# Recurrence output stored once in float32 and split where it is loaded, and a gates' slab loaded ahead of the block's moves

## What is computed

```
u_lru, g_lru, q, k, v, gate_lru, gate_attn = split(x @ w_in + b_in)
u     = depthwise_conv(u_lru)
h     = scan of h[t] = a[t] * h[t-1] + bt[t], forward and backward; a and bt from gates(u)
y_lru = ((h_fwd + h_bwd) * gelu(g_lru)) @ w_lru_out          # D_RNN = 1280
y_att = windowed_gqa(q, k, v) @ w_attn_out
mix   = (sigmoid(gate_lru) * y_lru + sigmoid(gate_attn) * y_att) @ w_o
x     = layer_norm(ALPHA * x + mix)
out   = layer_norm(ALPHA * x + gated MLP(x))                 # D_FF = 3072
```

## Time and profile before

| | us |
|---|---|
| median of 3 runs | 2767.41 (2765.99 to 2768.99) |
| the profiled execution | 2770.9 |
| its span (first to last instruction) | 2769.1 |
| PE busy in the span | 2671.8 |
| phase lru of q = 0 | about 0 to 376 |
| phase lru of q = 1 | about 1845 to 2024 |

### The profile page before, as it was taken

One profiled execution on the slowest core, in us unless ns is written; L12 is line 12 of the kernel. 1 busy time (PEld: TensorE's weight loads), 2 busy tenths in 40 slices (PEclk: granted clock), 3 DMA queues, 4 the chain that ended last, 5 costly groups with the idle time before them and its releaser, 6 DMA issues.

```text
span 2769.1 us, 32046 instructions
## 1 busy us (share of the span) xinstructions
PE 2671.8 (96%) x11898; PEld 2202.5 (80%) x11898; DVE 1506.4 (54%) x1800; ACT 753.4 (27%) x1033; POOL 654.1 (24%) x332
## 2 busy tenths in 40 slices
PE   8997999999899999999999999989999999999998
PEld 6886788888678877888888888878788778888886
DVE  7899864334313657745445464667742314644445
ACT  4565713313210022010101011148831211211112
POOL 3554531231133612334343433310000000000000
PEclk9998999999899999999999999999999999999999
DMA  6565654444686833434343534357756794544554
GB/s 232 183 204 185 213 193 160 172 157 159 262 353 231 301 125 137 137 137 153 136 179 128 188 124 161 132 215 235 244 186 228 256 343 159 205 183 182 192 201 168
DMA packets 174272, 535.67 MB, mean 193 GB/s; under 512 B 13863, under 2 KB 40743, under 8 KB 172112
## 3 DMA queue, kind: packets, MB, share of 16 engines
q1 hardware_dynamic: 116992, 430.94, 43.1%
q10 hardware_dynamic: 57168, 103.21, 10.5%
HBM read 310.99 MB, written 214.19 MB: 190 GB/s over the span
## 4 chain that ended last, share of the span: by engine, by line
PE 82%; DVE 9%; DMA 4%; ACT 2%; issue 1%; POOL 1%; ACTq 0%; SPq 0%; DVEq 0%; POOLq 0%
PE ps L857 48%; PE ps L1176 12%; PE ps L1003 8%; PE ps L1097 4%; PE ps L907 3%; PE ps L1036 2%; PE ps L986 2%; DMA gate_in<-gate_dram 1%; DMA W<-w_split 1%; PE ps L1023 1%; PE ps L910 1%; PE ps L1165 1%; DVE tau L1750 1%; DMA al_dram<-AOL 0%; DMA w_split<-W 0%
## 5 line engine op out<-in xcount | busy, mean ns | idle before, releaser
L857 PE MATMUL ps<-XH,W 128*128 128x512 f32 x4224 | 1208.2, 392 | 24.9 <-DVE XL L1695 11.6
L857 PEld LDWEIGHTS ps<-XH,W 128*128 128x128 f32 x4224 | 798.0, 189 | 202.1 <-issue 18.4
L857 PE MATMUL ps<-XL,W 128*128 128x512 f32 x2112 | 712.1, 391 | 0.0
L857 PEld LDWEIGHTS ps<-XL,W 128*128 128x128 f32 x2112 | 399.2, 189 | 83.1
L1176 PE MATMUL ps<-W,HH 128*128 128x512 f32 x1152 | 310.4, 389 | 1.7 <-DVE HL L2006 1.5
L1176 PEld LDWEIGHTS ps<-W,HH 128*128 128x128 f32 x1152 | 216.1, 188 | 47.3 <-DVE HL L2006 1.9
L741 POOL TENSOR_SCALAR W<-raw 128x1024 fp32r<-128x1024 f32 (+2 forms) x72 | 95.4, 1325 | 587.2 <-PE ps L857 277.6
L1003 PE MATMUL ps<-XH,W 128*128 128x512 f32 x672 | 216.4, 393 | 0.0
L807 POOL TENSOR_SCALAR W<-raw 128x1024 fp32r<-128x1024 f32 x72 | 87.4, 1213 | 535.3 <-PE ps L857 224.9
L742 POOL TENSOR_TENSOR W<-raw,W 128x1024 fp32r<-128x1024 f32 (+2 forms) x72 | 200.5, 2785 | 6.0
L808 POOL TENSOR_TENSOR W<-raw,W 128x1024 fp32r<-128x1024 f32 x72 | 191.9, 2666 | 6.0
(11 more groups left out here) (203 smaller groups left out, 3360.6 us busy)
## 6 DMA issues: line engine op xcount, KB each, us to landing
w_split<-W SPq DMA_DIRECT2D x131, 1024.0 KB, 6.4
W<-w_split SPq DMA_DIRECT2D x130, 1024.0 KB, 6.9
raw<-w_mlp SPq DMA_DIRECT2D x72, 512.0 KB, 4.9
raw<-w_qkv_mix SPq DMA_DIRECT2D x28, 512.0 KB, 3.9
w_split<-W SPq DMA_DIRECT2D x8, 1280.0 KB, 12.0
W<-w_split SPq DMA_DIRECT2D x8, 1280.0 KB, 7.7
gate_dram<-mix_out ACTq DMA_DIRECT2D x16, 512.0 KB, 2.7
gate_in<-gate_dram ACTq DMA_DIRECT2D x16, 512.0 KB, 6.2
```

The lines of the kernel that those rows point to most:

```text
L857: last = nc.tensor.matmul(bank(group, c), lhs(wl, k), rhs(xl, k, c), start=(k == 0 and n == 0), stop=(k == nk - 1 and n == 2))
```

## The change

- `store_y` stores one float32 tile in place of two; DVE's cast and subtraction behind the gelu multiplication are gone, and the wait for the store of the tile before now stands ahead of that multiplication. The count of `y_stored` is 16 for a tile.
- `load_y` loads the float32 tiles into the tail's buffer only. At the end of the phase attn ACT copies each into the head's buffer (`heads_of_y`, behind its last attention store) and DVE subtracts in place (`tails_of_y`, behind its last attention tail). PE waits for DVE's subtraction of each k tile. In q = 0 tiles 8 and 9 are handled behind the phase's end, in q = 1 all ten ahead of it.
- In q = 0 a gates' slab with jj >= 1 is loaded ahead of `moves_of_block`. For jj = 1 the stacking for block 1 comes next (`stack_second`), and the moves of block 0 with their wait only behind the save. For jj > 1 the moves stand between the load and the save. In q = 1 the order of SP's work stays.

```diff
@@ store_y @@
-            eng.dma_start(yh_dram[q][tile, :, :], tau[number % 2][1][:, 0:T]).then_inc(y_stored[q], 16)
-            eng.dma_start(yl_dram[q][tile, :, :], tau[number % 2][0][:, 0:T]).then_inc(y_stored[q], 16)
+            eng.dma_start(y_dram[q][tile, :, :], tau[number % 2][0][:, 0:T]).then_inc(y_stored[q], 16)
@@ SP, q = 0, loop over order_lru @@
+                def stack_second(q, T, h):
+                    sp.wait_ge(slab_done, first_slab(q, "lru") + slab_at[("gates", h, 0)] + 3)
+                    stack_rests(sp, q, T, h, 1)
                 def moves_of_block(q, T, h, jj):
-                    if jj == 0:
-                        sp.wait_ge(slab_done, first_slab(q, "lru") + slab_at[("gates", h, jj)] + 3)
-                        stack_rests(sp, q, T, h, jj + 1)
-                        if h:
-                            sp.wait_ge(scan_done[q], 2 * REST_TILE + 4)
+                    if h and jj == 0:
+                        sp.wait_ge(scan_done[q], 2 * REST_TILE + 4)
...
-                    if kind == "gates" and jj:
-                        moves_of_block(0, T, h, jj - 1)
                     if kind == "gates":
                         load(n, n % 2, A["w_gate"][HALF * h + jj, :, :], GATEW)
...
+                    if kind == "gates" and jj > 1:
+                        moves_of_block(0, T, h, jj - 1)
+                    if kind == "gates" and jj == 1:
+                        stack_second(0, T, h)
                     if n >= 2:
                         save(n - 2, n % 2, width_of[n - 2])
...
+                    if kind == "gates" and jj == 1:
+                        moves_of_block(0, T, h, 0)
@@ load_y @@
-                    for i in range(BLOCKS // 2):
-                        for dst, src in zip(X[q], (yh_dram, yl_dram)):
-                            for k in (2 * i, 2 * i + 1):
-                                sp.dma_start(dst[:, k, 0:T].bitcast(F32), src[q][k, :, :]).then_inc(y_in[i][q], 16)
+                    for k in range(BLOCKS):
+                        sp.dma_start(X[q][1][:, k, 0:T].bitcast(F32), y_dram[q][k, :, :]).then_inc(y_in[k // 2][q], 16)
@@ PE, y_ready_of @@
-                        if kk % 2 == 0:
-                            pe.wait_ge(y_in[kk // 2][q], 64 if kk < BLOCKS else 32)
+                        pe.wait_ge(y_split[q], kk + 1)
@@ ACT @@
+                    def heads_of_y(part):
+                        for k in part:
+                            act.wait_ge(y_in[k // 2][q], 32 if k < BLOCKS else 16)
+                            A1(y_tile(q, 0, k, T), y_tile(q, 1, k, T).bitcast(F32), ACT.Copy).then_inc(y_head[q], 1)
...
                         store(nb - 1)
+                    heads_of_y(range(RT if q else BLOCKS))
...
                     end_phase(act, end_of(q, "attn"))
...
                     if q == 0:
+                        act.dma_start(YR[q][1][:, :, 0:T].bitcast(F32), y_dram[q][BLOCKS:RT, :, :].rearrange("k p t -> p k t")).then_inc(y_in[4][q], 16)
                         load_gate(0)
                         load_gate(1)
+                        heads_of_y(range(BLOCKS, RT))
@@ DVE, recur @@
-                        order(V.tensor_tensor(tau_j[0], tau_j[0], gate, ALU.mult))
-                        dve.wait_ge(y_stored[q], 32 * (n + 1))
-                        order(V.tensor_copy(tau_j[1].bitcast(F32R), tau_j[0]))
-                        tell(V.tensor_tensor(tau_j[0].bitcast(F32R), tau_j[0], tau_j[1], ALU.subtract),
-                             y_ready[q], n + 2)
+                        dve.wait_ge(y_stored[q], 16 * (n + 1))
+                        tell(V.tensor_tensor(tau_j[0], tau_j[0], gate, ALU.mult), y_ready[q], n + 2)
@@ DVE, end of attn @@
+                    def tails_of_y(part):
+                        for k in part:
+                            dve.wait_ge(y_head[q], k + 1)
+                            tell(V.tensor_tensor(y_tile(q, 1, k, T), y_tile(q, 1, k, T).bitcast(F32),
+                                                 y_tile(q, 0, k, T).bitcast(F32), ALU.subtract), y_split[q], k + 1)
...
+                    tails_of_y(range(RT if q else BLOCKS))
                     end_phase(dve, end_of(q, "attn"))
+                    if q == 0:
+                        tails_of_y(range(BLOCKS, RT))
```

More of the change, by code:

```diff
@@ L300, in build @@
         gate_dram = [scratch(f"gate_dram{q}", (16, P, T)) for q, T in enumerate(SEQS)]
-        yh_dram = [scratch(f"yh_dram{q}", (RT, P, T)) for q, T in enumerate(SEQS)]
-        yl_dram = [scratch(f"yl_dram{q}", (RT, P, T)) for q, T in enumerate(SEQS)]
+        y_dram = [scratch(f"y_dram{q}", (RT, P, T)) for q, T in enumerate(SEQS)]
         ah_dram = [scratch(f"ah_dram{q}", (HEADS, P, T)) for q, T in enumerate(SEQS)]
@@ L388, in build @@
         ao_stored = [PerSeq(f"ao_stored{i}") for i in range(3)]
+        y_head = PerSeq("y_head")
+        y_split = PerSeq("y_split")
         at_in = PerSeq("at_in")
@@ L534, in out_count, with y_tile @@
             return 2 * (q + 1), sum(T // P - 2 for T in SEQS[:q + 1])
+        def y_tile(q, t, k, T):
+            return X[q][t][:, k, 0:T] if k < BLOCKS else YR[q][t][:, k - BLOCKS, 0:T]
         def end_of(q, phase):
@@ L642, in load_y @@
                 def load_y(q, T):
-                    sp.wait_ge(y_stored[q], 32 * (RT + 1))
+                    sp.wait_ge(y_stored[q], 16 * (RT + 1))
                     sp.wait_ge(slab_done, first_slab(q, "y_lru") + 2)
-                    for i in range(BLOCKS // 2):
-                        for dst, src in zip(X[q], (yh_dram, yl_dram)):
-                            for k in (2 * i, 2 * i + 1):
-                                sp.dma_start(dst[:, k, 0:T].bitcast(F32), src[q][k, :, :]).then_inc(y_in[i][q], 16)
+                    for k in range(BLOCKS):
+                        sp.dma_start(X[q][1][:, k, 0:T].bitcast(F32), y_dram[q][k, :, :]).then_inc(y_in[k // 2][q], 16)
                     if q:
-                        for dst, src in zip(YR[q], (yh_dram, yl_dram)):
-                            sp.dma_start(dst[:, :, 0:T].bitcast(F32), src[q][BLOCKS:RT, :, :].rearrange("k p t -> p k t")).then_inc(y_in[4][q], 16)
+                        sp.dma_start(YR[q][1][:, :, 0:T].bitcast(F32), y_dram[q][BLOCKS:RT, :, :].rearrange("k p t -> p k t")).then_inc(y_in[4][q], 16)
                 two_at_a_time("attn", A["w_qkv_mix"], D_MODEL, D_MODEL)
@@ L695, in _ @@
                         sp.dma_start(gs[:, :].bitcast(F32), gs_dram[blk, :, :]).then_inc(stack_in, 16)
+                        if jj == 1:
+                            stack_second(1, T, h)
                         if jj:
@@ L1265, in _ @@
                 for q, T in enumerate(SEQS):
-                    for s, n in ((gate_evac, gate_banks(T)), (rest_moved, 64), (y_stored, 32)):
+                    for s, n in ((gate_evac, gate_banks(T)), (rest_moved, 64), (y_stored, 16)):
                         act.sem_inc(s[q], n)
@@ L1316, in decays @@
                         for d in range(2):
-                            act.wait_ge(y_stored[q], 32 * n)
+                            act.wait_ge(y_stored[q], 16 * n)
                             A1(tau[n % 2][d][:, 0:T], r[d], ACT.Tanh, scale=decay_n[:, bass.ds(d * RT + tile, 1)]).then_inc(decay_done[q], 1)
@@ L1511, in _ @@
                     end_phase(act, end_of(q, "attn"))
-                    for dst, src in zip(YR[q], (yh_dram, yl_dram)) if q == 0 else ():
-                        act.dma_start(dst[:, :, 0:T].bitcast(F32), src[q][BLOCKS:RT, :, :].rearrange("k p t -> p k t")).then_inc(y_in[4][q], 16)
                     if q == 0:
+                        act.dma_start(YR[q][1][:, :, 0:T].bitcast(F32), y_dram[q][BLOCKS:RT, :, :].rearrange("k p t -> p k t")).then_inc(y_in[4][q], 16)
                         load_gate(0)
                         load_gate(1)
+                        heads_of_y(range(BLOCKS, RT))
                     def load_attention(i):
@@ L1816, in _ @@
                             split_values()
-                            dve.wait_ge(y_stored[q], 32 * (RT + 1))
+                            dve.wait_ge(y_stored[q], 16 * (RT + 1))
                         for n in range(1, 6):
```

## The result

| | before | after |
|---|---|---|
| median | 2766.32 us (11 runs) | 2773.69 us (11 runs) |
| ratio to before, 95% interval | | 1.0022 [1.0014, 1.003] |
| profiled execution, its span | 2770.9, 2769.1 | 2773.7, 2771.9 |

What follows compares the result with a forecast made beforehand. TensorE bounds the kernel, busy 2671.8 of 2769.1 us. The terms -4.4 - 4.0 - 2.0 + 5.0 + 2.0 sum to -3.4 us, so the median becomes 2764.0 us, range 2757.5 to 2771.

Steps and rivals of the forecast that it cites:

- the term taken back for POOL: Block (1, 1), first sequence: POOL's next slab falls beside VectorE's scan, so 1.7 us of the gain go back.
- The four waits of 1.1 us: First sequence's recurrence, slabs with jj = 2 and 3: TensorE's four waits for POOL vanish, gain 4.4 us, between 0 and 4.4.
- the load ahead does nothing: Rival: POOL is held by the slot's save, so the four 1.1 us waits stay; +1.0, 2768.4 us, chance 0.14.
- In the changed order the load and its companion go out long before, during SP's wait: First sequence's slabs with jj = 2 and 3: the save then goes 1.10 us earlier, the length of the wait.
- Block (1, 1): First sequence: earlier load and lighter VectorE bring the third gate tile forward, 4.0 us gained, between 0 and 7.0.
- Second sequence's recurrence: Fewer VectorE operations shorten TensorE's 4.48 us sigmoid wait at block (1, 1): 2.0 us gained, between 0 and 4.5.
- Moved y wait and stores: VectorE's multiplication waits for the previous tile's store: costs nothing while stores land in time, at most 0.2 us once.
- End of attention, first sequence: TensorE waits for the first y tile behind nearly free store issues: 5.0 us lost, between 4.35 and 10.2.
- End of attention, second sequence: Late start of y @ w_lru: 3.4 us with a free issue, 6.2 blocked; 2.0 us loss taken, between 0 and 5.
- Free, it ends at 2203.6: Second sequence's end of attention: the second store issue, 3.33 us before, is free; the y tile is ready at 2205.0.
- a later start falls partly into these waits: Behind the second sequence's y @ w_lru: TensorE's waits shrink by at least 1.39 us when it starts later.
- the store issue stays blocked: Rival: ScalarE's last stores block 6.36 and 3.33 us, deciding in the first sequence; +4.1, 2771.5 us, chance 0.22.

Runs made afterwards that it cites:

- y alone: The changed kernel with SyncE's old order in the recurrence, y still stored once and split where it is loaded: 2773.08 us, ratio 1.0019 to before.
- the order alone: The kernel before with SyncE's new order alone, both y halves stored and loaded as before: 2767.75 us, ratio 0.9998 to before.
- the best version: The changed kernel with early y tiles, ScalarE's last two stores behind the copies and SyncE's old order at block (0, 1): 2758.35 us, ratio 0.9969 to before.
- the second trace: The changed kernel measured again, nothing altered, on the same chip as the two runs beside it: 2772.84 us, ratio 1.002 to before.

## Why the prediction was wrong

The step that turned the sign is the end of attention of the second sequence: priced at +2.0 us with a free store issue and a late start partly absorbed, it cost +6.9, because the issue in front of ScalarE's copies blocked. Beside it, the slab of block (0, 1) had no price and cost 1.4, and the term taken back for POOL was too small. Term by term:

*The four waits of 1.1 us* (-4.4). Right in its mechanism, and nearly in its size: all four are gone, and done alone this gives 3.9 us. The rival that the load ahead does nothing falls with it.

*"In the changed order the load and its companion go out long before, during SP's wait"*: this failed for block (0, 1), which had no place in the sum at all. There SyncE's wait for POOL's raw slot is the long one, and stacking and moves came to stand behind it. Measured +1.4 us up to that slab (44.26 against 42.90), all of it given back in the run with the old order there (42.90); the other 0.6 us of the bill lie ahead of the first gates' slab, where the kernels do the same work. The front of the text said that jj = 1 has an order of its own; the prediction priced jj = 1 by block (1, 1) only and took the load as a thing without a wait.

*Block (1, 1)* (-4.0). The mechanism was right to the instruction: the third tile, the scan, the sigmoid. From (1, 0) to (1, 2) the change gave 3.4 us, of which 1.1 belong to the waits above: -2.3. The mis-sized term is the 1.7 us taken back for POOL: measured from the beginning of block (1, 0), it is 4.4. The prediction looked only at the slab behind, whose split stretches two operations by 2.7 us; the gates' slab's own split, moved by the early load, stretches four more by 3.2, and 1.5 us of delay further on go away. Against this the lighter VectorE gives 7.7 us at the scan, not 5.9. Only 0.7 of the 2.77 us of the long cast were saved, since the operation now beside POOL takes 3.30 us in place of 1.22; but others that had been long beside POOL became short, such as the scan itself, at 2.29 us in place of 3.50 in the first direction. The early load, to which half of the argument went, gives nothing here: y alone had -2.2 in this stretch, the order alone +3.3, and the old order in the best version was as fast as the new. The Trainium skill ("SBUF — State Buffer", section "SBUF: two separate sides") gave by its rule 2.7 us for this block, nearer than my 4.0, and the trace agrees with it: 1.95 and 3.26 us beside POOL, 1.23 and 1.23 without, each long one ending 1.1 us after an instruction of POOL's.

*Second sequence's recurrence* (-2.0): -2.9, within its bounds; 1.9 of it is at the wait that was named, 2.57 us in place of 4.48. *Moved y wait and stores* (0): no row speaks against it.

*End of attention, first sequence* (+5.0): +5.1, and luck has a part in it. The issues were free and only the first tile was waited for, as forecast. But the reason given, a backlog that is over when the issue comes, is not what happened: the forecast set the backlog's end near 742 against an issue at the old time, and the issue came at 735.67, with the backlog still there (share 1.10 until about 739). It was free all the same, and why is open. And 0.6 us are ScalarE's wait for a landing, which no term held; in the second trace that wait and the loss are larger, 5.8 us. The Trainium skill's rule that issuing takes little ("DMA: Bandwidth & Descriptors", section "Issuing engines are not separate DMA queues") holds at this place, with 0.37 and 0.57 us, and fails at the next, with 3.15.

*End of attention, second sequence* (+2.0): +6.9 at the place (+5.9 in the second trace). Two sentences of it failed. "Free, it ends at 2203.6": no row was given for a free issue here, and it blocked for 3.15 us. The blocked value, 6.2 us, stood in the text and was nearly the true one, yet the bounds, 0 to 5, left it out. And "a later start falls partly into these waits": the experiment that delayed the start by 3.9 us showed no shrinking behind it, and the bill has +1.2 us there in one trace and -1.2 in the other, which is scatter. The 1.39 us wait of before did go away, but others of VectorE's z_kept stayed, 4.9 us in all against 5.2 (5.1 in the second trace). That the transfers of this full stage follow TensorE's progress, so that a delayed TensorE delays them, fits both runs; no run varied them by themselves.

The rival "the store issue stays blocked" was half right: at the second sequence, not at the first, where it was said to decide. It gave 2771.5 and its place at 2203 a price of 2.3 us on top of the sum's 2.0; the measured one was 4.9. That 2773.69 came out near it is chance: it decided in the first sequence, where its mechanism was absent. Taken by steps, -3.4 becomes +5.7 by +4.9 there, +1.4 at block (0, 1), +1.7 at block (1, 1), -0.9 and +0.1 in the second recurrence and at the first end of attention, +0.2 at the four waits, and +1.2 and +0.6 at the end and the start, where the traces scatter by as much (the steps are rounded).

## What to carry to other kernels

Before work is put behind an engine's last stores, look at how long the issues take at each such place, every sequence for itself, and price them so unless a row shows them free; the DMA share does not tell (1.10 beside a free issue, 1.06 beside a blocked one). An issue that blocks costs nothing until something wanted stands behind it, and moving one statement can be worth more than the change. When a load is moved ahead of other issues of the same queue, ask what the load itself waits for: everything moved behind it inherits that wait. Ask too which engine works on what was loaded, and beside what it will now work. A start that is late by some microseconds should be charged in full, unless a row shows what it would otherwise wait for that does not depend on it.

## What the runs showed of the hardware

VectorE operations of 1.23 us took 1.95 and 3.26 us while POOL split a slab, and the cure, one wait on POOL, was worth 3.5 us in the trace and 5 us between the medians 2758.35 and 2753.26: an idle engine's work, done as early as it can be, was on the critical path through the operations beside it. And the issue of a store of one size took 0.57 us in one sequence and 3.15 in the other, with DMA shares of 1.10 and 1.06 around them; full DMA engines alone do not make an issue block.
